# Two-column matmuls in place of small transposes, and another order of work around the adaLN modulation, in a one-core diffusion layer

## The chip, the cores and the metric

The kernel runs on one core of a Trainium2 chip. A core has TensorE (matmuls; in the profile PE, and PEld for its weight loads), VectorE (DVE), ScalarE (ACT), GpSimd (POOL) and SyncE (SP, which issues most transfers here). Each engine works through its own list of instructions in order, and the lists are tied together by semaphores. The metric is the device time of one execution in microseconds (us), as the median of several.

## The reference, cut to what matters

One layer of a diffusion backbone: an RMSNorm whose result is scaled and shifted by vectors computed from a conditioning vector (adaLN), one wide input projection, two attention branches, their merge and an output projection. There are 1024 latent tokens and 256 prompt tokens, 1024 features, all in f32. The change touches only the modulation at the start:

```python
def _modulation(cvec, w_ada, b_ada):
    m = jax.nn.silu(cvec) @ w_ada + b_ada
    return m[..., :D_MODEL], m[..., D_MODEL:2 * D_MODEL], m[..., 2 * D_MODEL:]   # shift, scale, gate

def _project(x, shift, scale, w_in):
    h = _rmsnorm(x) * (1.0 + scale) + shift
    p = h @ w_in
    ...
```

There are two conditioning vectors, one for the latent tokens and one for the prompt tokens, so every modulation value exists twice.

## The kernel before

Matrix products are done in split form. An f32 operand is written as a high part rounded to fp32r and a low part (the f32 value less the high part), and three fp32r matmuls (high by high, high by low, low by high) add up to the product (`split_mm`, L82 to L87, whose matmul is L86). ScalarE writes high parts, VectorE low parts.

The function `front` computes modulation, normalised activations, keys and values of branch B and the values of branch A. The order is written out by hand, one list for each engine:

- *Loads (SP).* A ring of eight 512 KB slots takes the adaLN weights (8 blocks of 128 rows for the shift half, 8 for the scale half), then the key weights, then six pieces of the value weights. Then come x tiles, tables and so on.
- *Modulation matmuls (TensorE, `modulation`).* With the SiLU of the two conditioning vectors as weights, blocks 0, 2, 4, 6 of each half go in split form (L313: four rows come out, namely the two products with the high parts of the vectors and the two with the low parts), and the others as ordinary f32 matmuls (L319: two rows). The results stand as 4 x 512 rows in two PSUM banks for each half: rows 0 and 1 the one sum, rows 2 and 3 the rest, for the two vectors.
- *Rows to columns (`columns`).* The modulation is needed with features along the partitions. ScalarE (L506, L514) and VectorE (L652) copy the rows to SBUF (`modrow`, shown in traces as h), TensorE transposes each 4 x 128 block to 128 x 4 (L334, into mod_ps), and VectorE adds the bias (L646, L655) and then columns 2 and 3 (L649, L659) into `modf`. columns(0) is the shift half, columns(1) the scale half.
- *Chunks.* For each of 8 feature blocks of a token group TensorE transposes the normalised x (`transposed`, L345, two banks in turn), ScalarE applies scale and shift (`modulate`, L453), VectorE writes high and low part (`parts`, L578 and L580), and TensorE runs the key matmuls of that block (`keys_chunk`, L353). ScalarE's chunk i waits for the low part of chunk i - 2, and x chunk i for ScalarE's chunk i - 2.
- *Value weights.* `values_high(m)` (ScalarE, L444) and `values_low(m)` (VectorE, L570) split the six pieces. The first value matmuls (`value_unit`, `split_mm`) need pieces 0 to 2 and all eight chunks.

The two semaphores that order this place are mod_row (rows copied to SBUF) and mod_col (a half transposed); mod_ready counts VectorE's adds into `modf`. After `front` come the attention pairs (`pairs`) and the merge (`finish`), which the change leaves alone.

Of the kernel before, what the change touches and what calls it, by code (L numbers as in the profile page):

```python
# [37 lines left out]
ALU = mybir.AluOpType  # L38
# [3 lines left out]
P = 128  # L42
D = 1024
KD = D // P
# [45 lines left out]
def front(nc, io, block, left, right, right_later, ident, scol, hm, wv, wkb, wt, wraw, craw, w_in, w_hi, w_lo):  # L90
# [12 lines left out]
    mod_ps, t_ps, k_ps, v_ps = (right_later[n] for n in ("mod_ps", "t_ps", "k_ps", "v_ps"))  # L103
    junk = left["junk"]
    scl = left["scl"]
    modrow = h32[0:4, :, :]
# [196 lines left out]
    @block.tensor  # L303
    def _(pe):
        def modulation(half, k):

            n = (SHIFT, SCALE)[half] + k
            if (half, k) in SPLIT:
                j = SPLIT.index((half, k))
                pe.wait_ge(mod_lo, j + 1)  # L310
                for c in range(2):
                    for part in range(2):
                        mm = pe.matmul(v_ps[0:4, 2 * half + c, :], scl[:, k, :], mod_part(j, part)[:, c * 512:(c + 1) * 512],  # L313
                                       start=(k == 0 and part == 0), stop=False, skip_group_check=True)
                mm.then_inc(ada_used, 1)
                return
            ring_wait(pe, n)
            for c in range(2):
                mm = pe.matmul(v_ps[0:2, 2 * half + c, :], scol[:, k, :], ring(n)[:, c * 512:(c + 1) * 512],  # L319
                               start=False, stop=(k == KD - 1), skip_group_check=True)  # L320
                if k == KD - 1:
                    mm.then_inc(mod_mm, 1)
            if k < KD - 1:
                mm.then_inc(ada_used, 1)

        def columns(half):

            if half == 1:
                pe.wait_ge(mod_ready, 2)
            for b in range(KD):  # L330
                if b % 4 == 0:
                    pe.wait_ge(mod_row, 2 * half + b // 4 + 1)
                blk = half * KD + b
                mm = pe.transpose(mod_ps[:, 4 * blk:4 * blk + 4], modrow[:, b // 4, (b % 4) * P:(b % 4 + 1) * P],  # L334
                                  ident[0:4, 0:4])
            mm.then_inc(mod_col, 1)

        def transposed(i):

            g, k = CHUNK[i]  # L340
            pe.wait_ge(xn_done, XG[g][0] + XG[g][1])
            if i >= 2:
                pe.wait_ge(h_done, i - 1)
            for t in range(XG[g][1]):
                mm = pe.transpose(t_ps[:, i % 2, t * P:(t + 1) * P], x(g)[:, t, k * P:(k + 1) * P], ident[:, :])  # L345
            mm.then_inc(xt_done, 1)

        def keys_chunk(g, k):

            t0, n = tokens(g)  # L350
            pe.wait_ge(lo_done, g * KD + k + 1)
            for i, (a, b) in enumerate(((0, 0), (0, 1), (1, 0))):
                mm = pe.matmul(k_ps[:, 0:n], wkb[:, a, k * P:(k + 1) * P], hm[:, b, k, t0:t0 + n],  # L353
                               start=(k == 0 and i == 0), stop=(k == KD - 1 and i == 2))
            if k == KD - 1:
                mm.then_inc(k_mm, 1)

        def value_unit(u):

            t, n = UNITS_V[u]  # L360
            if u == 0:
                pe.wait_ge(wv_lo, 3)
            if u == 4:
                pe.wait_ge(wv_lo, 6)
            pe.wait_ge(lo_done, KD * (1 if t < 4 else 2 if t < 8 else 3))
            if u >= 4:
                pe.wait_ge(v_lo, u - 3)
            split_mm(pe, v_ps[:, u % 4, 0:HW], lambda a, k: hm[:, a, k, t * P:(t + 1) * P],
                     lambda b, k: wv[:, b, k, n * HW:(n + 1) * HW], KD).then_inc(mm_done, 1)

        def gate_sum():

            pe.wait_ge(g_acc, 2 * KD)
            pe.wait_ge(const_set, 4)
            pe.wait_ge(h_done, len(CHUNK))
            for c in range(2):
                for s in range(2):
                    mm = pe.matmul(t_ps[0:2, c, :], pick[:, 2 * s:2 * s + 2], gacc[:, s, c * 512:(c + 1) * 512],
                                   start=(s == 0), stop=(s == 1))
            mm.then_inc(g_mm, 1)  # L380

        pe.wait_ge(scl_done, 2)
        for half, k in MODS:
            if (half, k) == (1, 6):
                pe.wait_ge(ident_in, 16)
                columns(0)
                transposed(0)
                transposed(1)
            modulation(half, k)
        columns(1)  # L390
        pe.wait_ge(wk_lo, 1)
        for k in range(KD):
            if k + 2 < KD:
                transposed(k + 2)
            keys_chunk(0, k)
        for u in range(3):
            value_unit(u)
        for j in range(4):
            transposed(KD + 2 * j)
            transposed(KD + 2 * j + 1)  # L400
            value_unit(3 + j)
        value_unit(7)
        pe.wait_ge(k_raw, 1)
        for k in range(KD):
            keys_chunk(1, k)
        for j in range(4):
            value_unit(8 + j)
            transposed(2 * KD + 2 * j)
            transposed(2 * KD + 2 * j + 1)
        for u in range(12, 16):  # L410
            value_unit(u)
        pe.wait_ge(k_raw, 2)
        for k in range(KD):
            keys_chunk(2, k)
        value_unit(16)
        value_unit(17)
        value_unit(18)
        gate_sum()
        value_unit(19)
        pe.wait_ge(k_raw, 3)  # L420
        pe.wait_ge(g_row, 2)

    @block.scalar
    def _(act):
# [16 lines left out]
        def values_high(m):  # L441

            ring_wait(act, VALUES + m)
            act.activation(values_split(m, 0), values_raw(m), ACT.Copy).then_inc(wv_hi, 1)  # L444

        def modulate(i):

            g, k = CHUNK[i]
            n, stream = XG[g][1] * P, int(g == 2)
            act.wait_ge(xt_done, i + 1)  # L450
            if i >= 2:
                act.wait_ge(lo_done, i - 1)
            act.activation(h32[:, i % 2, 0:n], t_ps[:, i % 2, 0:n], ACT.Identity,  # L453
                           bias=modf[:, k, stream:stream + 1], scale=modf[:, KD + k, stream:stream + 1]
                           ).then_inc(h_done, 1)
# [52 lines left out]
        ring_wait(act, KEYS)  # L508
        act.activation(wkb[:, 0, :], ring(KEYS), ACT.Copy).then_inc(wk_hi, 1)
        values_high(0)  # L510
        values_high(1)
        act.wait_ge(mod_mm, 3)
        act.wait_ge(mod_col, 1)
        act.activation(modrow[:, 0, :], v_ps[0:4, 2, :], ACT.Copy).then_inc(mod_row, 1)  # L514
        values_high(2)
        act.wait_ge(mod_ready, 4)
        for i in range(KD):
            modulate(i)
        for t in range(XG[1][1]):
            square(1, t)  # L520
        root(1)
# [25 lines left out]
    def _(dve):  # L547
# [19 lines left out]
        def values_low(m):  # L567

            dve.wait_ge(wv_hi, m + 1)
            dve.tensor_tensor(values_split(m, 1), values_raw(m), values_split(m, 0).bitcast(F32), ALU.subtract  # L570
                              ).then_inc(wv_lo, 1)
# [55 lines left out]
                    dve.scalar_tensor_tensor(out=gacc[:, s, :], in0=wgate(kg)[:, :], scalar=scol[:, kg, s:s + 1],  # L627
                                             in1=gacc[:, s, :], op0=ALU.mult, op1=ALU.add).then_inc(g_acc, 1)

        mods = mod_ps[:, 0:8 * KD].rearrange("p (b s) -> p b s", s=4)  # L630
        bias = bcol[:, :].rearrange("p (b o) -> p b o", o=1)
        dve.wait_ge(silu_done, 1)
        dve.tensor_copy(scl[:, :, 0:2], scol[:, :, :]).then_inc(scl_done, 1)
# [2 lines left out]
        for j in range(6):  # L636
# [2 lines left out]
        mod_low(7)  # L639
        dve.wait_ge(wk_hi, 1)  # L640
        dve.tensor_tensor(wkb[:, 1, :], ring(KEYS), wkb[:, 0, :].bitcast(F32), ALU.subtract).then_inc(wk_lo, 1)
        values_low(0)
        values_low(1)
        dve.wait_ge(small_in, 32)
        dve.wait_ge(mod_col, 1)
        dve.tensor_tensor(modf[:, 0:KD, :], mods[:, 0:KD, 0:2], bias[:, 0:KD, :].to_broadcast([P, KD, 2]), ALU.add  # L646
                          ).then_inc(mod_ready, 1)
        dve.wait_ge(mod_ready, 1)
        dve.tensor_tensor(modf[:, 0:KD, :], modf[:, 0:KD, :], mods[:, 0:KD, 2:4], ALU.add).then_inc(mod_ready, 1)  # L649
        dve.wait_ge(mod_mm, 4)  # L650
        dve.wait_ge(mod_row, 3)
        dve.tensor_copy(modrow[:, 1, :], v_ps[0:4, 3, :]).then_inc(mod_row, 1)  # L652
        values_low(2)
        dve.wait_ge(mod_col, 2)
        dve.scalar_tensor_tensor(out=modf[:, KD:, :], in0=mods[:, KD:, 0:2], scalar=1.0,  # L655
                                 in1=bias[:, KD:, :].to_broadcast([P, KD, 2]), op0=ALU.add, op1=ALU.add
                                 ).then_inc(mod_ready, 1)
        dve.wait_ge(mod_ready, 3)
        dve.tensor_tensor(modf[:, KD:, :], modf[:, KD:, :], mods[:, KD:, 2:4], ALU.add).then_inc(mod_ready, 1)  # L659
        for i in range(KD):  # L660
            parts(i)
        normalise(1)
        for m in range(3, 6):
            values_low(m)
# [1445 lines left out]
```

## Time and profile before

| | |
|---|---|
| median of 3 runs | 1246.5 us (1246.5 to 1248.01) |
| the profiled execution | 1246.5 us |
| its span, first to last instruction | 1244.7 us |
| mean granted TensorE clock | 0.995 |
| TensorE matmul busy | 1208.9 us (97%), 7488 instructions |
| TensorE weight loads | 1086.3 us (87%) |
| VectorE | 843.0 us (68%) |
| ScalarE | 613.5 us (49%) |
| GpSimd | 191.9 us (15%) |

Busy time is a share of the span. TensorE's weight loads overlap its matmuls. Matmuls are pipelined, so the duration of one is longer than the distance from its start to the next one's; where a price of one matmul is wanted, the distance between starts is the one to take. The chain of waits in the profile puts 75% of the span on TensorE and 13% on VectorE. In the profile's 40 slices TensorE is busy six tenths of the first (0 to 31 us), and nine tenths or more of all others but the last.

### The profile page before, as it was taken

The page shows a single profiled execution, that of the slowest core. Times are in us where ns is not written, and L with a number is a line of the kernel's source. Part 1 is how long each engine was busy: PE and PEld are TensorE (multiplying, and loading weights), DVE is VectorE, ACT ScalarE, POOL GpSimd, SP SyncE. Part 2 cuts the span into 40 slices and gives each one's busy share as a digit, 9 for nine tenths or more (in the row PEclk, how much of TensorE's full clock was granted, in tenths as well). Part 3 has the DMA queues.
Part 4 walks back from the last instruction along what each step waited for, and adds up shares of the span by engine and source line. Part 5 has one row for each costly group of instructions (what it writes and reads, how often), then busy time and mean ns, then how long its engine had stood idle before and what let it go on. Part 6 is the DMA issues. An engine that isn't in the chain of part 4 may idle for free.

```text
span 1244.7 us, 21419 instructions
## 1 busy us (share of the span) xinstructions
PE 1208.9 (97%) x7488; PEld 1086.3 (87%) x7488; DVE 843.0 (68%) x1654; ACT 613.5 (49%) x1217; POOL 191.9 (15%) x203
## 2 busy tenths in 40 slices
PE   6999999999999999999999999999999999999997
PEld 1699889988998998899889889989988888998996
DVE  3669458766766776687687687678768876454452
ACT  5532335534553555355466456555547574443341
POOL 0000214121302221141000000000000024533430
PEclk9999999999999999999999999999999999999999
DMA  9447523132214213222511111411013277543530
GB/s 365 146 185 219 202 88 102 58 133 83 93 62 136 87 63 121 84 93 76 168 62 39 54 56 39 126 43 62 18 51 111 72 238 250 174 151 115 200 138 34
DMA packets 81116, 143.03 MB, mean 115 GB/s; under 512 B 7047, under 2 KB 58119, under 8 KB 81037
## 3 DMA queue, kind: packets, MB, share of 16 engines
q1 hardware_dynamic: 66636, 119.92, 28.9%
q10 hardware_dynamic: 14400, 22.15, 4.9%
q8 instruction: 38, 0.62, 0.2%
q14 instruction: 42, 0.34, 0.1%
HBM read 106.65 MB, written 35.40 MB: 114 GB/s over the span
## 4 chain that ended last, share of the span: by engine, by line
PE 75%; DVE 13%; issue 5%; ACT 4%; DMA 2%; ACTq 0%; SPq 0%; DVEq 0%; POOL 0%
PE d_ps_pairs L86 20%; PE y_ps L1836 9%; PE b_ps L86 9%; PE s_ps_pairs L86 8%; PE o_ps_pairs L1069 7%; PE t_ps_pairs L1038 6%; PE v_ps L86 6%; PE s_ps_pairs L997 3%; PE s_ps_pairs L996 3%; DVE pt L1388 2%; DVE mn L1398 1%; DVE s_ps_pairs L1405 1%; PE k_ps L353 1%; ACT pr L1194 1%; DVE pr L1454 1%
## 5 line engine op out<-in xcount | busy, mean ns | idle before, releaser
L86 PE MATMUL d_ps_pairs<-h,wt 128*128 128x384 f32 (+2 forms) x1920 | 352.3, 338 | 0.5 <-ACT craw L1212 0.5
L86 PEld LDWEIGHTS d_ps_pairs<-h,wt 128*128 128x128 f32 x1920 | 316.7, 188 | 15.6 <-ACT craw L1212 1.0
L1388 DVE TENSOR_TENSOR pt<-t_ps_pairs,pt 128x512 fp32r<-128x512 f32 (+1 forms) x272 | 157.6, 621 | 38.7 <-ACT pt L1170 37.4
L86 PE MATMUL s_ps_pairs<-h,wt 128*128 128x512 f32 (+1 forms) x864 | 169.3, 355 | 0.5 <-DVE q L1345 0.5
L1194 ACT ACTIVATE pr<-s_ps_pairs,mx 128x896 f32<-128x896 f32 x128 | 128.3, 1005 | 70.3 <-DVE mx L1414 40.8
L86 PEld LDWEIGHTS s_ps_pairs<-h,wt 128*128 128x128 f32 x864 | 141.7, 189 | 23.0 <-DVE q L1345 1.1
L1170 ACT ACTIVATE pt<-t_ps_pairs 128x512 fp32r<-128x512 f32 (+1 forms) x272 | 134.1, 548 | 14.7 <-PE t_ps_pairs L1038 9.9
L1038 PE MATMUL t_ps_pairs<-ident_sb,pr 128*128 128x128 f32 x960 | 131.7, 275 | 4.0 <-DVE pt L1388 2.8
L1038 PEld LDWEIGHTS t_ps_pairs<-ident_sb,pr 128*128 128x128 f32 x960 | 107.7, 140 | 15.7 <-DVE pt L1388 11.4
L1836 PE MATMUL y_ps<-wo,mg 128*128 128x512 f32 x480 | 113.2, 396 | 0.0
L1790 POOL TENSOR_TENSOR tp<-tp 128x256 f32<-128x256 f32 x40 | 32.3, 808 | 497.7 <-DVE tp L1888 497.1
L1836 PEld LDWEIGHTS y_ps<-wo,mg 128*128 128x128 f32 x480 | 90.0, 188 | 21.6
L1398 DVE TENSOR_REDUCE mn<-s_ps_pairs 128x2 f32<-128x1024 f32 x64 | 78.1, 1220 | 36.3 <-PE s_ps_pairs L997 35.0
L947 POOL TENSOR_TENSOR comb_a<-rowm_a,comb_a 128x384 f32<-128x384 f32 x48 | 45.4, 945 | 318.1 <-DMA comb_a<-in_bias 318.1
L86 PE MATMUL b_ps<-og,wb 128*128 128x256 f32 x720 | 87.7, 282 | 1.6 <-DVE tp L1888 1.6
L86 PEld LDWEIGHTS b_ps<-og,wb 128*128 128x128 f32 x720 | 86.8, 188 | 1.9 <-DVE wb L1565 1.0
L1454 DVE TENSOR_SCALAR pr<-pr,rden 128x896 f32<-128x896 f32 x128 | 87.0, 722 | 2.2
L1243 ACT ACTIVATE otmp<-o_ps_pairs 64x256 f32<-64x256 f32 (+1 forms) x72 | 29.2, 405 | 117.0 <-PE o_ps_pairs L1069 116.5
L1212 ACT ACTIVATE craw<-d_ps_pairs 128x384 f32<-128x384 f32 (+2 forms) x80 | 39.0, 488 | 74.5 <-PE d_ps_pairs L86 74.4
L86 PE MATMUL v_ps<-wv,h 128*128 128x320 f32 x480 | 73.1, 310 | 0.0
L86 PEld LDWEIGHTS v_ps<-wv,h 128*128 128x128 f32 x480 | 70.7, 188 | 1.0 <-issue 0.9
L1888 DVE TENSOR_TENSOR tp<-b_ps,gt 128x256 f32<-128x256 f32 x80 | 31.9, 420 | 46.0 <-PE b_ps L86 33.2
(184 smaller groups left out, 1722.3 us busy)
## 6 DMA issues: line engine op xcount, KB each, us to landing
wraw<-in_w_gate SPq DMA_DIRECT2D x24, 512.0 KB, 3.4
gt<-gates_d SPq DMA_DIRECT2D x40, 256.0 KB, 4.5
comb_a<-in_bias SPq DMA_DIRECT2D x24, 384.0 KB, 3.6
gates_d<-craw ACTq DMA_DIRECT2D x48, 192.0 KB, 1.9
vw_a<-v_d SPq DMA_DIRECT2D x64, 128.0 KB
v_d<-vst SPq DMA_DIRECT2D x20, 320.0 KB, 4.5
wada<-in_w_ada SPq DMA_DIRECT2D x12, 512.0 KB, 8.8
oz<-gates_d SPq DMA_DIRECT2D x20, 256.0 KB, 4.7
```

Source lines behind the costliest of these rows:

```text
L86: mm = eng.matmul(out, lhs(a, k), rhs(b, k), start=(k == 0 and i == 0), stop=(k == n_k - 1 and i == 2))
L947: pool.tensor_tensor(c, rm, c, ALU.subtract).then_inc(comb_t, 1)
L996: pe.matmul(out, cols(q1[:, h, :]), rhs(h, slice(0, P)), start=True, stop=False)
L1038: mm = pe.transpose(t_ps[:, n % 2, b * P:(b + 1) * P], probs_block(s, t, kb), ident[:, :])
L1069: mm = pe.matmul(o_ps[:, c0 * P:(c0 + nb) * P], v, pt[:, part, b0 * P:(b0 + nb) * P], start=(half == 0 and part == 0 and (n == 0 or (s == ...
L1170: act.activation(pt[:, 0, c * 512:c * 512 + cols], t_ps[:, n % 2, 0:cols], ACT.Copy).then_inc(hi_done, 1)
L1194: act.activation(probs_run(s, t), scores_run(s, t), ACT.Exp, bias=mx[:, t:t + 1], scale=-1.0, accum_out=den[:, t:t + 1]).then_inc(exp_done, 1)
L1212: act.activation(gst[:, u % 2, 0:n], d_ps[:, 0:n], ACT.Copy).then_inc(g_done, 1)
L1388: dve.tensor_tensor(pt[:, 1, c * 512:c * 512 + cols], t_ps[:, n % 2, 0:cols], pt[:, 0, c * 512:c * 512 + cols].bitcast(F32), ALU.subtract) ...
L1398: dve.tensor_reduce(mn[:, 0:2], s_ps[:, :, :].rearrange("p (t b) c -> p t b c", b=2)[:, :, s % 2, :], AX.X, ALU.min).then_inc(m1_done, 1)
L1454: dve.tensor_scalar(probs_run(s, t), probs_run(s, t), rden[:, t:t + 1], None, ALU.mult).then_inc(p_done, 1)
L1836: mm = pe.matmul(y_ps[:, e, n * 512:(n + 1) * 512], mg[:, a, k, e * P:(e + 1) * P], wo[k][:, b, n * 512:(n + 1) * 512], start=(k == 0 and ...
```

## The change

In `columns`, each 4 x 128 block is no longer transposed by the transpose operation with the 4 x 4 identity. Two matmuls with two columns of the identity each write the same two columns of mod_ps, the second adding to the first; so rows 0 and 2, and 1 and 3, are summed in PSUM. VectorE's two adds L649 and L659 go, with the waits around them. The order around it changes in all three lists.

```diff
             if half == 1:
-                pe.wait_ge(mod_ready, 2)
+                pe.wait_ge(mod_ready, 1)
...
-                mm = pe.transpose(mod_ps[:, 4 * blk:4 * blk + 4], modrow[:, b // 4, (b % 4) * P:(b % 4 + 1) * P],
-                                  ident[0:4, 0:4])
+                for part in range(2):
+                    mm = pe.matmul(mod_ps[:, 2 * blk:2 * blk + 2], modrow[:, b // 4, (b % 4) * P:(b % 4 + 1) * P],
+                                   ident[0:4, 2 * part:2 * part + 2], start=(part == 0), stop=(part == 1))
...
                 columns(0)
-                transposed(0)
-                transposed(1)
             modulation(half, k)
+        transposed(0)
         columns(1)
+        transposed(1)
...
         values_high(0)
-        values_high(1)
         act.wait_ge(mod_mm, 3)
         act.wait_ge(mod_col, 1)
         act.activation(modrow[:, 0, :], v_ps[0:4, 2, :], ACT.Copy).then_inc(mod_row, 1)
-        values_high(2)
-        act.wait_ge(mod_ready, 4)
+        values_high(1)
+        act.wait_ge(mod_ready, 2)
         for i in range(KD):
             modulate(i)
+            if i == 1:
+                values_high(2)
...
-        values_low(0)
-        values_low(1)
         dve.wait_ge(small_in, 32)
         dve.wait_ge(mod_col, 1)
-        dve.tensor_tensor(modf[:, 0:KD, :], mods[:, 0:KD, 0:2], bias[:, 0:KD, :].to_broadcast([P, KD, 2]), ALU.add
+        dve.tensor_tensor(modf[:, 0:KD, :], mods[:, 0:KD, :], bias[:, 0:KD, :].to_broadcast([P, KD, 2]), ALU.add
                           ).then_inc(mod_ready, 1)
-        dve.wait_ge(mod_ready, 1)
-        dve.tensor_tensor(modf[:, 0:KD, :], modf[:, 0:KD, :], mods[:, 0:KD, 2:4], ALU.add).then_inc(mod_ready, 1)
         dve.wait_ge(mod_mm, 4)
         dve.wait_ge(mod_row, 3)
         dve.tensor_copy(modrow[:, 1, :], v_ps[0:4, 3, :]).then_inc(mod_row, 1)
-        values_low(2)
         dve.wait_ge(mod_col, 2)
-        dve.scalar_tensor_tensor(out=modf[:, KD:, :], in0=mods[:, KD:, 0:2], scalar=1.0,
+        dve.scalar_tensor_tensor(out=modf[:, KD:, :], in0=mods[:, KD:, :], scalar=1.0,
                                  in1=bias[:, KD:, :].to_broadcast([P, KD, 2]), op0=ALU.add, op1=ALU.add
                                  ).then_inc(mod_ready, 1)
-        dve.wait_ge(mod_ready, 3)
-        dve.tensor_tensor(modf[:, KD:, :], modf[:, KD:, :], mods[:, KD:, 2:4], ALU.add).then_inc(mod_ready, 1)
+        values_low(0)
+        values_low(1)
         for i in range(KD):
             parts(i)
+        values_low(2)
```

TensorE's list, from the last but one split modulation block of the scale half to the first key matmuls, before (v_ps holds modulation rows, mod_ps the modulation in columns, t_ps the transposed x, k_ps the keys):

```order
L313 MATMUL v_ps<-h,scl 4x512 x4
L334 MATMUL mod_ps<-ident_sb,h 128x4 x8
L345 MATMUL t_ps<-ident_sb,x 128x128 x8
L313 MATMUL v_ps<-h,scl 4x512 x4
L319 MATMUL v_ps<-x,scol 2x512 x2
L334 MATMUL mod_ps<-ident_sb,h 128x4 x8
L345 MATMUL t_ps<-ident_sb,x 128x128 x4
L353 MATMUL k_ps<-h,wkb 128x512 x3
```

and the same place now:

```order
L313 MATMUL v_ps<-h,scl 4x512 x4
L335 MATMUL mod_ps<-ident_sb,h 128x2 x16
L313 MATMUL v_ps<-h,scl 4x512 x4
L319 MATMUL v_ps<-x,scol 2x512 x2
L346 MATMUL t_ps<-ident_sb,x 128x128 x4
L335 MATMUL mod_ps<-ident_sb,h 128x2 x16
L346 MATMUL t_ps<-ident_sb,x 128x128 x8
L354 MATMUL k_ps<-h,wkb 128x512 x3
```

Each set of 8 has become 16 instructions, and the first two x chunks have moved from ahead of the last two modulation blocks to either side of the second set.

VectorE's list from the key weights' low part to the first chunk, before (wkb key weights, wv value weights, modf the modulation, h as output of L652 the copied rows and of L578 and L580 the parts of the chunk):

```order
L641 TENSOR_TENSOR wkb<-wada,wkb 128x1024
L570 TENSOR_TENSOR wv<-wada,wv 128x3x320 x2
L646 TENSOR_TENSOR modf<-mod_ps,bcol 128x16
L649 TENSOR_TENSOR modf<-modf,mod_ps 128x16
L652 COPY h<-v_ps 4x512
L570 TENSOR_TENSOR wv<-wada,wv 128x2x320
L655 SCALAR_TENSOR_TENSOR modf<-mod_ps,bcol 128x16
L659 TENSOR_TENSOR modf<-modf,mod_ps 128x16
L578 CAST h<-h 128x512
```

and now:

```order
L643 TENSOR_TENSOR wkb<-wada,wkb 128x1024
L646 TENSOR_TENSOR modf<-mod_ps,bcol 128x16
L650 COPY h<-v_ps 4x512
L652 SCALAR_TENSOR_TENSOR modf<-mod_ps,bcol 128x16
L572 TENSOR_TENSOR wv<-wada,wv 128x3x320 x2
L580 CAST h<-h 128x512
L582 TENSOR_TENSOR h<-h 128x512
```

The first two value weight pieces moved from ahead of L646 to between the last add and the first chunk; the third now stands behind the last of the eight chunks.

## Rows read from the trace of the kernel before

**Rows 1.** Chain of waits: start us, us, what.

```profile
33.88 0.58 PE mod_ps L334 x8
...
38.94 0.73 DVE wv L570
...
52.55 10.57 PE v_ps L86 x72
```

**Rows 2.** Timeline, TensorE: start us, us, instruction, [idle before it <- released by].

```profile
33.81 0.65 PE L334 MATMUL mod_ps<-ident_sb,h 4*128 4x4 f32 x8
34.39 1.09 PE L345 MATMUL t_ps<-ident_sb,x 128*128 128x128 f32 x8
35.24 1.17 PE L313 MATMUL v_ps<-h,scl 128*4 128x512 f32 x4
...
38.15 0.40 PE L334 MATMUL mod_ps<-ident_sb,h 4*128 4x4 f32 x4
...
42.01 1.65 PE L353 MATMUL k_ps<-h,wkb 128*128 128x512 f32 x3 [0.47 <-DVE h L580]
...
45.47 0.60 PE L345 MATMUL t_ps<-ident_sb,x 128*128 128x128 f32 x4
45.83 0.94 PE L353 MATMUL k_ps<-h,wkb 128*128 128x512 f32 x3
...
46.96 0.95 PE L353 MATMUL k_ps<-h,wkb 128*128 128x512 f32 x3
47.75 0.60 PE L345 MATMUL t_ps<-ident_sb,x 128*128 128x128 f32 x4
...
52.39 10.73 PE L86 MATMUL v_ps<-wv,h 128*128 128x320 f32 x72
```

**Rows 3.** The same timeline, VectorE.

```profile
33.78 1.16 DVE L570 TENSOR_TENSOR wv<-wada,wv 128x960 fp32r<-128x960 f32 x1
...
38.26 0.68 DVE L652 COPY h<-v_ps 4x512 f32<-4x512 f32 x1 [1.68 <-PE v_ps L319]
...
39.60 0.15 DVE L655 SCALAR_TENSOR_TENSOR modf<-mod_ps,bcol 128x16 f32<-128x16 f32 x1
39.79 0.17 DVE L659 TENSOR_TENSOR modf<-modf,mod_ps 128x16 f32<-128x16 f32 x1
40.80 0.43 DVE L578 CAST h<-h 128x512 fp32r<-128x512 f32 x1 [0.85 <-ACT h L453]
...
50.84 0.69 DVE L580 TENSOR_TENSOR h<-h 128x512 fp32r<-128x512 f32 x1
55.30 0.18 DVE L552 RECIPROCAL rstd<-rms 128x4 f32<-128x4 f32 x1 [3.76 <-ACT rms L438]
...
58.17 2.22 DVE L570 TENSOR_TENSOR wv<-wada,wv 128x960 fp32r<-128x960 f32 x2
60.31 0.82 DVE L570 TENSOR_TENSOR wv<-x,wv 128x640 fp32r<-128x640 f32 x1
```

**Rows 4.** The same timeline, ScalarE.

```profile
37.40 0.59 ACT L514 ACTIVATE h<-v_ps 4x512 f32<-4x512 f32 x1 [2.30 <-PE v_ps L319]
37.89 0.72 ACT L444 ACTIVATE wv<-wada 128x640 fp32r<-128x640 f32 x1
39.99 1.45 ACT L453 ACTIVATE h<-t_ps,modf 128x512 f32<-128x512 f32 x2 [1.38 <-DVE modf L659]
```

**Rows 5.** Busy time by stretch, behind the first value matmul: stretch, length, engines, clock, DMA.

```profile
52.40:130.00 77.60, 77.60 (x533) 76.47 (x532) 57.60 (x95) 28.53 (x55) 0.00 (x0) 1.00 0.50 163
```

**Rows 6.** Line L319, its matmul records: duration ns min/median/max, first and last start, forms.

```profile
L319 PE MATMUL v_ps<-wada,scol x24: 591/592/1015, 9.7 to 32.3; 128*2 128x512 f32 x24
...
L319 PE MATMUL v_ps<-x,scol x8: 591/592/592, 23.6 to 37.6; 128*2 128x512 f32 x8
```

**Rows 7.** Busy time by stretch, around the first key matmul.

```profile
38.55:42.00 3.45, 1.03 (x9) 0.74 (x8) 2.54 (x7) 1.51 (x3) 0.00 (x0) 0.99 1.02 408
42.00:45.40 3.40, 3.39 (x10) 2.78 (x11) 2.06 (x5) 1.55 (x2) 0.00 (x0) 0.51 0.23 89
```

More of the change, by code:

```diff
@@ L628, in gate_product @@
                                              in1=gacc[:, s, :], op0=ALU.mult, op1=ALU.add).then_inc(g_acc, 1)
-        mods = mod_ps[:, 0:8 * KD].rearrange("p (b s) -> p b s", s=4)
+        mods = mod_ps[:, 0:4 * KD].rearrange("p (b s) -> p b s", s=2)
         bias = bcol[:, :].rearrange("p (b o) -> p b o", o=1)
```

## The prediction

> **What bounds the kernel now.** I read the chain of waits first. It runs through the whole span, and up to the first key projection its links are one serial line: the load of the adaLN weights, TensorE's modulation matmuls, then in turn ScalarE, VectorE and TensorE with little on any of them. The part that the change touches lies in it piece by piece (some of them in [rows 1]): the eight small transposes of L334, the eight x transposes of L345, the last modulation matmuls (L319), VectorE's row copy (L652), a weight split (L570, 0.73 us) that only stands in front of L655 in VectorE's queue, then L655, L659, ScalarE's first modulated chunk (L453), VectorE's two parts of it (L578, L580) and the first key matmuls at 42.01. Second I read the timelines of TensorE, VectorE and ScalarE over 33 to 53 us [rows 2 to 4], for who is late where. Third I looked at what follows: from 52.4 to 130 us TensorE is busy the whole time [rows 5], and everything else waits for it or has room. So whatever the front loses or wins ahead of the first value matmul (52.39) moves the rest as a block, and reaches the end: after that point nothing in the order changes. The profiled execution took 1246.5 us, which is the median of the three; its span is 1244.7, so 1.8 us lie outside.
>
> **What the edits are, priced one at a time.** I name moments by the trace before and carry a shift d.
>
> 1. *First set of small products, columns(0).* Before: 8 transposes, from 33.81 to the next start at 34.39: 0.58 us, 0.0725 each with their 4x128 weight load [rows 2]. Now each block is two ordinary f32 matmuls of two columns, which add the high and low rows in PSUM: 16 matmuls. The trace shows what an ordinary f32 matmul costs in records: L319 issues two per k over 8 such k, which is 16, and the two rows of L319 count 24 + 8 = 32 [rows 6]. So 16 matmuls are 32 weight loads and 32 array passes, where a transpose was one record. No row shows such a record at 128x2. Bounds: from above the 128x128 transpose of L345, 0.85 us for 8 or 0.106 each, which loads 128 weight columns and streams 128; farther above, L86 at 10.57/72 = 0.147 [rows 1]; from below, the pair of records at the price of one L334, 0.036 each. L334 itself has the same weights (4 rows, 128 columns) and nearly no moving columns, so I take 0.0725: 32 x 0.0725 = 2.32 us, +1.74. It is on the path, because TensorE runs without an idle time from 33.81 to 38.15.
>
> 2. *x transposes moved behind the modulation matmuls.* The 8 of L345 at 34.39 took 0.85 us ahead of the last two modulation steps [rows 2]: -0.85. The last modulation result, which VectorE waited for at 38.26, now comes at 38.26 + 1.74 - 0.85 = 39.15; TensorE's stream behind it goes on at 39.04 (38.15 before).
>
> 3. *Second set, columns(1).* transposed(0) now stands ahead of it: 4 of those transposes, 0.43 us, to 39.47. The first half needs ScalarE's row copy (L514, 0.59 us [rows 4]), which shifts by 0.89 to end at 38.88; the second needs VectorE's (L652, 0.68), 39.15 to 39.83; TensorE comes to it at 39.47 + 1.16 = 40.63. Neither waits. 32 x 0.0725 = 2.32 ends at 41.79; with 0.07 for the last pass to finish and 0.04 to hand over, L655 starts at 41.90. Before it started at 39.60 and was followed by L659; L659 goes (-0.19 from start to start), and so does the split of 0.73 us in front of L655. The modulation is ready at 42.05 against 39.96, and ScalarE's first chunk starts at 42.08 against 39.99: d = +2.09. The three savings (0.85, 0.73, 0.19) are real but come to 1.77 us against 3.9 us more of matmul records.
>
> 4. *Two weight splits moved behind L655.* values_low(0) and (1) ran at 33.78 and 35.13, while VectorE had nothing to do: it sat idle 1.68 us before L652 [rows 3]. Now they stand between L655 and the parts of the first chunk. Two such splits take 2.14 us from the start of one pair to what follows it (58.17 to 60.31 [rows 3]). From 42.03 they end at 44.17; the first chunk is ready from ScalarE at 42.08 + 0.81 = 42.89 (39.99 to 40.80 before) and waits 1.3 us. The cast L578 starts at 44.17 against 40.80: d = +3.4. Queued behind it are the keys' first matmuls, which need L580, and ScalarE's third chunk, which needs the same. The first key matmul moves from 42.01 to 45.4.
>
> 5. *The rest costs nothing.* ScalarE's values_high(1) (half as wide again as values_high(2), which took 0.72 [rows 4], so about 1.1 us) goes into its wait between L514 and the modulation (38.9 to 42.1); uncovered it would cost 1.1. values_high(2) goes behind chunk 1, where ScalarE waits for L580 of chunk 0 anyway: chunk 1 ends near 43.6, that L580 near 45.4. VectorE's values_low(2) (0.80) now follows the last parts, which ended at 50.84 + 0.69 = 51.53, ready by 52.33; the first value matmul, which needs it, started at 52.39 after the last key chunk. That is a tie, at most +0.1. VectorE then waited 3.76 us for ScalarE's L438 [rows 3], so normalise(1) isn't late. L646 drops its follower L649 (0.20), off the path. The loads keep their order, and none of their releases depends on a moved instruction.
>
> Key chunks 0 to 7 took 42.01 to 52.39. Their pace is set by TensorE, ScalarE and VectorE in turn and nothing in their order changes, so d = +3.4 passes through: 1246.5 + 3.4 = **1249.9 us**, +0.27%.
>
> The row of L334 speaks against a rule of the skill: eight weight loads of 128 columns and eight passes went by in 0.58 us [rows 2]. The Trainium skill (TensorE: Matmul & The Clock Gate, "LDWEIGHTS (loading the stationary operand)") puts a weight load at the number of columns over 1.2, whatever the rows, which would be 107 ns here and more than the measured 72.5 ns for load and pass together. By that rule the sum would be about 1252, an estimate, as in the dear case below; by the row it is 1249.9.
>
> **Rivals.**
>
> *The clock holds through the key chunks.* Granted clock was 0.51 from 42.0 to 45.4, after 3.45 us in which TensorE was busy 1.03 [rows 7]; so the first two key chunks and the transposes between them ran at the 1.2 GHz level: 42.01 to 45.47 is 3.46 us, where the same three pieces one lap later (key chunk 46.96 to 47.75, transposes 45.47 to 45.83) are 0.79 + 0.36 + 0.79 = 1.94 [rows 2]. Now TensorE works from 39.04 to about 42.8 and then idles some 2 us before the first key matmul. For: TensorE idles less than in the 3.45 us that went before the fall here. Against: there is still a gap, and the passes are tiny. If it holds, 1.5 us come back: d = +1.9, 1248.4, which is no change. This is the case on the other side: its place is the stretch of 42 to 48 us, its price 1.5, and it decides as soon as it gives back over 0.9 us. With cheap records (next but one) on top d would be -0.45, 1246.0.
>
> *The small matmuls are dear.* At L345's 0.106 each set costs 1.07 more, both lie on the path: d = +3.4 + 2.1 = +5.5, 1252.0; at L86's 0.147, +8.2, 1254.7. For: two passes accumulate into the same two columns right behind each other, which the trace nowhere shows, and the clock may be at 1.2 GHz in part of them. Against: L334.
>
> *The small matmuls are cheap* (a pair for the price of one transpose, so the edit costs no TensorE time): each set 1.16 us less. The modulation would then be ready at 39.7, 0.2 before its old time, but the two splits still stand in the way: d = +3.4 - 2.3 = +1.1, 1247.6, no change.
>
> **Chances.** Forecast (d from 2.6 to 4.6) 0.52; clock holds 0.17; dear 0.16; cheap 0.08; cheap with the clock held, or something as good, 0.04; elsewhere 0.03. About 0.2% of the time, 2.5 us, is what a measurement can tell from no change. Slower: 0.52 + 0.16 + 0.03 = 0.71. The same: 0.17 + 0.08, less 0.01 for a part of them that goes lower still: 0.24. Faster: that 0.01 and the 0.04, 0.05 in all, since only these come near it. The range is 1247.5 (cheap) to 1252.8 (past L345's price): it leaves out the far end of the dear case and what lies under the cheap one. The forecast's own range is 1249.1 to 1251.1.
>
> **What the profile of the changed kernel would show.** Step 1: 32 records in the first set, about 2.3 us from its first start to the next matmul; 1.2 says cheap, 3.4 says dear. Step 2: VectorE's row copy near 39.2. Step 3: second set ends near 41.8, the one remaining add of the scale half starts near 41.9 and ScalarE's first chunk near 42.1. Step 4: two splits of 1.16 us between that add and the first cast, the cast near 44.2, while ScalarE's chunk 0 had ended 1.3 us earlier. Step 5: first key matmul near 45.4, first value matmul near 55.8, with no wait there for the split of VectorE; clock near 0.5 for some 3 us from the first key matmul on. I am wrong if the first value matmul comes within 2 us of 52.4, or if it comes at 55.8 and the end does not move with it, which would mean room later that I took for none.

## The result, and the profile after

The changed kernel took 1255.57 us (median, 1253.78 to 1256.91) against 1246.5 before: 1.0070 of the time, 95% interval 1.0052 to 1.0088, about 9 us slower. The forecast was slower too, but by 3.4 us, with a range that ended at 1252.8. The direction was right and the size wrong. The profiled execution took 1256.8 us (before: 1246.5), its span is 1254.9 us (1244.7).

TensorE's timeline after, at the place of [rows 2] (start us, us, instruction, records, idle before it):

```profile
33.20 1.09 PE L313 MATMUL v_ps<-h,scl 128*4 128x512 f32 x4
34.21 4.51 PE L335 MATMUL mod_ps<-ident_sb,h 4*128 4x2 f32 x32
38.65 1.87 PE L313 MATMUL v_ps<-h,scl 128*4 128x512 f32 x4
40.45 3.52 PE L319 MATMUL v_ps<-x,scol 128*2 128x512 f32 x4
43.90 0.66 PE L346 MATMUL t_ps<-ident_sb,x 128*128 128x128 f32 x4
44.49 4.54 PE L335 MATMUL mod_ps<-ident_sb,h 4*128 4x2 f32 x32
48.96 2.33 PE L346 MATMUL t_ps<-ident_sb,x 128*128 128x128 f32 x8
52.49 1.65 PE L354 MATMUL k_ps<-h,wkb 128*128 128x512 f32 x3 [1.21 <-DVE h L582]
...
63.61 2.69 PE L86 MATMUL v_ps<-wv,h 128*128 128x320 f32 x17
```

Each set has the 32 records that were foretold, but takes 4.44 and 4.47 us from start to start, not 2.32. And the modulation matmuls between the sets, which the change doesn't touch, take 5.25 us (38.65 to 43.90) where they took 2.91 (35.24 to 38.15 in [rows 2]). The granted clock tells why (busy time by stretch; the number after the five engines is the clock):

```profile
34.20:36.70 2.50, 2.50 (x24) 2.49 (x23) 0.00 (x0) 0.00 (x0) 0.00 (x0) 1.00 1.04 341
37.20:38.60 1.40, 1.40 (x8) 1.40 (x7) 0.00 (x0) 0.00 (x0) 0.00 (x0) 0.50 1.08 392
38.65:43.90 5.25, 5.25 (x9) 0.68 (x9) 0.17 (x1) 1.48 (x2) 0.00 (x0) 0.51 0.86 348
44.50:46.90 2.40, 2.40 (x23) 2.40 (x22) 0.19 (x1) 0.00 (x0) 0.00 (x0) 1.00 0.00 0
47.20:48.90 1.70, 1.70 (x10) 1.70 (x9) 0.00 (x0) 0.00 (x0) 0.00 (x0) 0.50 0.00 0
```

Inside each set the clock falls to its 1.2 GHz level, although TensorE is busy all the time (2.50 of 2.50 us before the fall, 1.40 of 1.40 behind it). After the first set the long modulation matmuls pay for it. VectorE, the place of [rows 3]:

```profile
38.83 0.17 DVE L646 TENSOR_TENSOR modf<-mod_ps,bcol 128x16 f32<-128x16 f32 x1 [4.99 <-PE mod_ps L335]
44.01 0.68 DVE L650 COPY h<-v_ps 4x512 f32<-4x512 f32 x1 [5.00 <-PE v_ps L319]
49.06 0.17 DVE L652 SCALAR_TENSOR_TENSOR modf<-mod_ps,bcol 128x16 f32<-128x16 f32 x1 [4.38 <-PE mod_ps L335]
49.15 2.22 DVE L572 TENSOR_TENSOR wv<-wada,wv 128x960 fp32r<-128x960 f32 x2
51.29 0.42 DVE L580 CAST h<-h 128x512 fp32r<-128x512 f32 x1
```

and ScalarE, of [rows 4]:

```profile
42.35 0.59 ACT L514 ACTIVATE h<-v_ps 4x512 f32<-4x512 f32 x1 [8.49 <-PE v_ps L319]
42.84 0.99 ACT L445 ACTIVATE wv<-wada 128x960 fp32r<-128x960 f32 x1
49.27 1.62 ACT L454 ACTIVATE h<-t_ps,modf 128x512 f32<-128x512 f32 x2 [5.44 <-DVE modf L652]
50.79 0.73 ACT L445 ACTIVATE wv<-wada 128x640 fp32r<-128x640 f32 x1
```

At each turn VectorE waits 4.4 to 5.0 us, and ScalarE 8.5 and 5.4 us: for TensorE's small matmuls, for what stands behind them, or for the add that waited for them. The two splits (L572) lie between the last add and the first cast as foretold.

### The profile page after: what moved, and what is told of

Its sections match the earlier page's. It is cut to its first block, busy times and chain, and to the rows that moved or that the text cites. A ratio compares the mean times of both kernels' runs of the same rounds, so it can differ in the third digit from the quotient of the medians.

```text
span 1254.9 us, 21513 instructions
## 1 busy us (share of the span) xinstructions
PE 1221.5 (97%) x7536; PEld 1095.1 (87%) x7536; DVE 843.2 (67%) x1652; ACT 613.6 (49%) x1217; POOL 192.1 (15%) x203
## 4 chain that ended last, share of the span: by engine, by line
PE 78%; DVE 12%; issue 4%; ACT 4%; DMA 1%; ACTq 0%; SPq 0%; DVEq 0%; POOL 0%
PE d_ps_pairs L86 19%; PE s_ps_pairs L86 11%; PE y_ps L1834 9%; PE b_ps L86 9%; PE o_ps_pairs L1067 7%; PE t_ps_pairs L1036 6%; PE v_ps L86 6%; PE s_ps_pairs L995 3%; PE s_ps_pairs L994 3%; DVE pt L1386 2%; DVE mn L1396 1%; DVE s_ps_pairs L1403 1%; ACT pr L1192 1%; PE v_ps L319 1%; PE k_ps L354 1%
```

## The experiments

Medians are compared with before's on the same chip (1246.24, 1246.13 and 1246.05 us in the three groups of runs). Single executions of before lie between 1243.1 and 1248.4, so a single execution tells a clock or the distance between two records, not a microsecond of total time. A good part of that spread arises before the change's place: in the thirteen profiles the first set of small products starts between 32.40 and 35.42 us, and what differs is the clock from 18 to 24 us. Where it stayed at 1.00 the set starts at 32.40 to 32.60 (four profiles); in the kernel before, with 0.50 and 0.64 over 18 to 22 us, at 33.81. Two profiles of one and the same kernel start it at 34.07 and 35.42. So the place is best compared from the start of its first set: up to the first value matmul it takes 18.58 us before (33.81 to 52.39) and 29.40 us after (34.21 to 63.61).

**The two halves of the change.** Matmuls alone: the edit of `columns` with VectorE's two adds gone, all orders as before.

> The order of before, with only the arithmetic of the change: two accumulating two-column f32 matmuls a block in place of one transpose, without VectorE's two adds. Theory A (the matmul records are the whole of it: 0.107 us each at the full clock and 0.21 at half, against 0.0725 for a transpose, and the modulation matmuls behind the first set then run at half clock too): the first set takes 3.4 to 4.5 us, the two modulation steps behind it about 5.3 instead of 2.9, the second set 3.4 or more; 7 to 10 us over before, about 1255, nearly all of the 9 us of the full change. Theory B (the new order costs the most, the split weights in front of the first chunk and x transposes in the wrong place): under 4 us over before, below 1250.5.

Order alone: the reverse.

```diff
-                for part in range(2):
-                    mm = pe.matmul(mod_ps[:, 2 * blk:2 * blk + 2], ...
+                mm = pe.transpose(mod_ps[:, 4 * blk:4 * blk + 4], ...
```

> The order of the change in all three lists, with the transposes and VectorE's four adds of before. Theory A: the modulation is ready about 1.1 us earlier, the two splits give back 1.3, so within 0.5 us of before, about 1246.8. Theory B (order): 4 us or more over before.

Measured: matmuls alone 1255.76 (1.0069, interval 1.0046 to 1.0091), order alone 1246.62 (1.0007, 0.9997 to 1.0016). The matmuls are the whole loss within what can be measured, and the order as a whole is free, because two of its parts cancel. In its profile ScalarE's first chunk starts 5.11 us after the first set (33.99 to 39.10) where it took 6.18 before (33.81 to 39.99), 1.07 less; then the two splits hold up the first cast, which comes 7.13 us after the set's start (41.12) against 6.99.

The single executions of the matmuls alone reach from 1248.86 us, at a mean granted clock of 0.997, to 1258.17 us, at 0.991. That is a spread of 9.3 us against 3.8 of before on the same chip: how much clock is lost differs from run to run. In its profile the sets take 4.34 and some 4.7 us.

**The place of the splits.** The full change with

```diff
         values_high(0)
+        values_high(1)
...
+        values_low(0)
+        values_low(1)
         dve.wait_ge(small_in, 32)
...
-        values_low(0)
-        values_low(1)
         for i in range(KD):
```

> The full change, but with the two value weight splits back ahead of the adds on VectorE, and the ScalarE half of the second ahead of the row copy. Step 4 of the prediction put 1.3 us on their place, and the trace after shows the first cast 1.2 us after its chunk is ready: 1.2 us faster than the changed kernel, about 1254.3. Rival: the key chunks run at half clock and TensorE is late anyway, so nothing comes back, 1255.6.

Measured 1254.17, but its ratio is 1.0076 (1.0059 to 1.0093) where the full change has 1.0070: inconclusive as a time. The trace is plain: the first cast comes 1.02 us after the last add instead of 2.23 (49.06 to 51.29). It reaches the first key matmul, which starts 2.33 us behind the second set (45.78 to 48.11) instead of 3.53 (48.96 to 52.49), which speaks against the rival.

```profile
45.88 0.18 DVE L654 SCALAR_TENSOR_TENSOR modf<-mod_ps,bcol 128x16 f32<-128x16 f32 x1 [4.35 <-PE mod_ps L335]
46.90 0.43 DVE L580 CAST h<-h 128x512 fp32r<-128x512 f32 x1 [0.84 <-ACT h L454]
```

This run also has a first set with the clock full to its end: 32.58 to 36.24, 3.66 us or 0.114 a record. The fall comes behind it, in L319:

```profile
32.58 3.73 PE L335 MATMUL mod_ps<-ident_sb,h 4*128 4x2 f32 x32
36.24 1.09 PE L313 MATMUL v_ps<-h,scl 128*4 128x512 f32 x4
37.26 3.56 PE L319 MATMUL v_ps<-x,scol 128*2 128x512 f32 x4
```

**What a record costs, and why.** Half as many of them, without accumulation, in the kernel before:

```diff
-                mm = pe.transpose(mod_ps[:, 4 * blk:4 * blk + 4], ..., ident[0:4, 0:4])
+                mm = pe.matmul(mod_ps[:, 4 * blk:4 * blk + 4], ..., ident[0:4, 0:4], start=True, stop=True)
```

> Order and adds of before, with one ordinary f32 matmul of four columns a block in place of the transpose (8 a set, so 16 records). Theory A1 (each record is bound by its weight load, 0.107 us at full clock): a set takes 1.7 us, 1.1 more than before, 2 to 4 us over before in all, about 1249. Theory A2 (the second matmul's accumulation into the same two columns is what is slow, the rest costs like a transpose): 16 records at 0.0725, 0.6 more a set, about 1247.5.

Measured 1248.32. One of the ten executions took 2060 us, at a mean granted clock of 0.592 against 0.994 to 0.996 in the others; what held its clock down is open. Without it the median is 1248.02, and the ratio 1.0014 (1.0000 to 1.0027). A set of 16 records took 1.88 us (34.75 to 36.63), 0.1175 each, with a full clock behind the first set, through the modulation matmuls:

```profile
34.75 1.94 PE L334 MATMUL mod_ps<-ident_sb,h 4*128 4x4 f32 x16
36.63 1.09 PE L345 MATMUL t_ps<-ident_sb,x 128*128 128x128 f32 x8
```

So accumulation isn't what is dear. Two matmuls a block without it confirm that:

```diff
-                mm = pe.transpose(mod_ps[:, 4 * blk:4 * blk + 4], ...
+                for part in range(2):
+                    mm = pe.matmul(mod_ps[:, 4 * blk + 2 * part:4 * blk + 2 * part + 2], ..., start=True, stop=True)
```

> Order and VectorE's adds of before; two ordinary f32 matmuls of two columns a block as in the change, but into separate columns, none adding to the other (32 records a set, nothing accumulated). Theory A1 (the weight load is the price of a record): 0.107 us a record at full clock as with accumulation, the clock falls as there, about 1255.8 as with the accumulating matmuls. Theory A2 (accumulating into the same columns is dear): records near 0.0725, about 1250.

Measured 1254.67 (1.0078, 1.0052 to 1.0104), as with accumulation, and 3.66 us for the first set (33.91 to 37.57), again 0.114 a record. Next, as many records of the cheap kind, each block transposed four times:

```diff
-                mm = pe.transpose(mod_ps[:, 4 * blk:4 * blk + 4], ...
+                for rep in range(4):
+                    mm = pe.transpose(mod_ps[:, 4 * blk:4 * blk + 4], ...
```

> Order and adds of before, each block transposed four times over into the same place, so 32 transpose records a set. It tells the number of records from their kind. Theory A1 (an ordinary f32 matmul's weight load is dearer than a transpose's): 0.0725 us each, 2.3 us a set. If short records by themselves make the clock fall, both sets and the modulation matmuls between show the half clock: 6 us or more over before, 1252.5. If the kind of record does, the clock is full there: about 3.5 us over before, 1249.8.

Measured 1249.1 (1.0027, 1.0017 to 1.0037). A set of 32 took 2.06 us, 0.064 each, all of it at full clock; but the clock fell right behind it, into the x transposes and the modulation step:

```profile
32.60:34.60 2.00, 2.00 (x33) 2.00 (x32) 1.88 (x2) 1.34 (x3) 0.00 (x0) 1.00 1.08 363
34.60:37.50 2.90, 2.90 (x14) 2.02 (x13) 1.92 (x4) 0.68 (x1) 0.00 (x0) 0.53 1.10 369
```

So a series of short records, transposes too, can be followed by the half clock; neither of my two readings in the expectation (clock full, or half in everything between) fits. Last, ordinary matmuls that are not f32: the rows rounded to fp32r as they are copied, into a free part of hm.

```diff
+    modr = lambda c: hm[0:4, 1, 2 * c:2 * c + 2, LAT:TOK]
...
+                    mm = pe.matmul(mod_ps[:, 2 * blk:2 * blk + 2], hm[0:4, 1, b // 2, ...], identr[:, 2 * part:2 * part + 2], ...
```

> Order of before with the accumulating two-column matmuls, but on fp32r operands: the copied rows are rounded to fp32r as they are written (so the modulation loses low bits, which is the part of the computation that changes), and the identity's four columns are copied once. 16 fp32r matmuls a set, one record each. Theory A1 (an ordinary f32 matmul is two records with a slow weight load each, the kind is what costs): 16 records at 0.07 us or a little more, 1.2 us a set, clock full, 0.5 to 1.5 us over before, about 1247. Rival (any matmul that isn't a transpose loads at 0.11 here): as the 16 records of the single f32 matmul, 1.9 us a set, 1248.3.

Measured 1248.91 (1.0027, 1.0015 to 1.0038), and 16 records in 1.87 us (32.40 to 34.27), 0.117 each:

```profile
32.40 1.94 PE L337 MATMUL mod_ps<-h 4*128 4x2 f32 x16
34.27 1.09 PE L348 MATMUL t_ps<-ident_sb,x 128*128 128x128 f32 x8
```

Here my theory fell and its rival held. It isn't f32 that makes a record slow: the small ordinary matmuls tried (128 weight columns, few streamed columns) took 0.114 to 0.118 us a record, a transpose of the same 4 x 128 block 0.064 to 0.073. That it is f32 only doubles the number of records.

**Does streaming more columns hold the clock?** 126 columns of the identity instead of 2 in the full change.

```diff
-    mod_ps[:, 2 * blk:2 * blk + 2], ..., ident[0:4, 2 * part:2 * part + 2]
+    mod_ps[:, 2 * blk:2 * blk + 126], ..., ident[0:4, 2 * part:2 * part + 126]
```

> The full change, but each of its small matmuls streams 126 columns of the identity in place of 2 (the further columns hold nothing that is used and are overwritten by the next block). Theory A1 (weight load and streaming overlap, and the load, 128 columns at 0.107 us, is the price): the record costs the same 0.107 at full clock. If the clock stays full with the array streaming, the 3.5 us that the half clock cost come back, about 1252; if it falls as before, 1255.6. Rival (the record's price is load plus stream): 0.21 a record, 6.8 us a set, 1259 or more.

Its profile showed the clock at 1.00 through both sets and all between (34.07 to 45.00), and a set at 3.76 us, 0.1175 a record: 63 times as many columns cost next to nothing, so the price isn't the streaming. What is left is the weight load or another cost of each record. The weight loads' own records differ as the prices do, a median of 187 ns for the ordinary matmul here and of 137 for the transpose of the same block four times over, and in both the loads follow each other without a gap (busy 3.64 of 3.66 us in the third experiment's first set, 2.00 of 2.00 in the transposes'):

```profile
L335 PEld LDWEIGHTS mod_ps<-ident_sb,h x64: 181/187/188, 34.1 to 44.7; 4*128 4x128 f32 x64
...
L335 PEld LDWEIGHTS mod_ps<-ident_sb,h x64: 133/137/140, 32.6 to 41.9; 4*128 4x128 f32 x64
```

(records of duration ns min/median/max, first and last start; the first line is of the wide columns, the second of the transposes four times over). That points to the weight load, but no run changed the number of weight columns, so it isn't shown.

The median was 1255.91 (1.0085, 1.0069 to 1.0101), no better than the change. Each of the two kernels was profiled once more:

> The full change with 126 streamed columns once more, for its clock alone. If streaming keeps the clock up, both sets and the modulation matmuls between them show 1.0 again, a set takes 3.8 us and the L313 step behind it 1.0; if the first profile was luck, the half clock shows in a set or right behind it.

> The changed kernel once more, for its clock alone. If the two-column records bring the clock down, the last part of a set and the modulation matmuls behind the first show 0.5 again, wherever the start falls; if its first profile was bad luck, they show 1.0 and the time is near 1252.

The wide one took 1260.29 us, with the clock at half in the very place; its first profile was luck:

```profile
34.41 1.09 PE L313 MATMUL v_ps<-h,scl 128*4 128x512 f32 x4
35.42 4.59 PE L335 MATMUL mod_ps<-ident_sb,h 4*128 4x126 f32 x32
39.94 1.87 PE L313 MATMUL v_ps<-h,scl 128*4 128x512 f32 x4
41.74 3.55 PE L319 MATMUL v_ps<-x,scol 128*2 128x512 f32 x4
```

The change once more took 1257.56 us, with sets of 4.85 and 4.87 us and again 1.87 for the L313 step behind the first. What the narrow matmuls lose in clock repeats in the second profile, its size varies, and wide columns don't cure it.

The lucky profile is worth more than it seems, since it shows the new matmuls with a full clock through both sets and all between. From the start of the first set to the first value matmul it takes 25.41 us (34.07 to 59.48). The same kernel with the clock fallen takes 29.62 (35.42 to 65.04), and the change 29.40 and 29.43: the clock costs 4.0 to 4.2 us there. The order alone, with transposes, takes 18.78 (33.99 to 52.77), so the records at full clock cost 6.6. These are single executions.

**A version that beats both.** The order-alone kernel with the two splits put back ahead; against the kernel before:

```diff
                 columns(0)
-                transposed(0)
-                transposed(1)
             modulation(half, k)
+        transposed(0)
         columns(1)
+        transposed(1)
...
-        values_high(2)
         act.wait_ge(mod_ready, 4)
         for i in range(KD):
             modulate(i)
+            if i == 1:
+                values_high(2)
...
-        values_low(2)
         dve.wait_ge(mod_col, 2)
...
             parts(i)
+        values_low(2)
```

> The version that the runs so far point to: transposes and VectorE's four adds of before, value weight splits 0 and 1 where they were, but the x transposes behind the last modulation matmuls, and the third split behind the last chunk. The first cast comes 1.05 us earlier than before (transposes 0.85 off the path, the split of 0.73 out of the way, less a wait for TensorE): 1245.2 by the trace. Rival: the idle stretch ahead of the key chunks stays and the half clock moves with it, so nothing shows at the end, 1246.3.

Measured 1243.86 us (0.9981, 0.9971 to 0.9990): faster than before by 1.2 to 3.6 us. In its profile the way from the first set to the first cast is 6.47 us (32.57 to 39.04) against 6.99 (33.81 to 40.80), only 0.5 shorter, because the second split holds up the row copy:

```profile
35.28 1.16 DVE L571 TENSOR_TENSOR wv<-wada,wv 128x960 fp32r<-128x960 f32 x1 [0.19 <-ACT wv L444]
36.36 0.17 DVE L647 TENSOR_TENSOR modf<-mod_ps,bcol 128x16 f32<-128x16 f32 x1
36.56 0.17 DVE L650 TENSOR_TENSOR modf<-modf,mod_ps 128x16 f32<-128x16 f32 x1
36.65 0.67 DVE L653 COPY h<-v_ps 4x512 f32<-4x512 f32 x1
39.04 0.43 DVE L579 CAST h<-h 128x512 fp32r<-128x512 f32 x1 [0.84 <-ACT h L453]
```

From the first set to the first value matmul it takes 18.13 us (32.57 to 50.70) against 18.58, again 0.45 less. Its first set starts 1.24 us earlier than before's, ahead of all that was changed, where the clock was 1.00 from 18 to 24 us. The mean granted clock of its eleven executions is 0.997 in the median, against 0.996 in before's twenty. That the median gains 2.3 us where the place explains 0.5 stays open. Against the third experiment, which differs from it only in `columns` and the adds, the matmuls cost 1254.17 - 1243.86 = 10.3 us (the two ran in different groups; before's medians there differ by 0.1).

## Why the prediction was wrong in size

*Step 1, the price of a small record, is the step that failed*, and with it a term that the sum put at nothing, the half clock in and behind the sets. The profiled execution lost 10.3 us and not 3.4. Of the 6.9 between them the price of a record is 2 x (3.66 - 2.32) = 2.7, and the clock 4.0 (29.40 less the 25.41 of the profile with a full clock there).

*The price.* I took 0.0725 us, from L334, because it has the same weights. Measured: 0.114 to 0.118 at full clock. The count of 32 was right. At full clock the first set costs 3.66 us, +3.1 and not +1.74. The nearest row was not the one with the same shape of weights but the one bound above, L345's 0.106, and even that was a little low. The Trainium skill's rule on weight loads (TensorE: Matmul & The Clock Gate, "LDWEIGHTS (loading the stationary operand)"), the number of columns over 1.2 whatever the rows, so an estimate of 107 ns for 128 columns, comes within about 10% of the ordinary matmuls here (114 to 118 ns), and not of the transposes (64 to 73 ns); I had tested it on a transpose and set it aside.

*The clock.* The rival with the clock only asked whether the old half-clock stretch would go. The reverse took place: the fall came earlier, in the middle of the set. In the profile after, the first set's 4.44 us hold 4.44 - 3.66 = 0.78 of it, and the untouched modulation matmuls behind it 5.25 - 2.91 = 2.34. I had named half clock inside the small matmuls as a reason for the dear case, and put no price on what stands behind them.

*Step 2* was right: the L313 step follows the set directly, -0.85. TensorE's stream behind the modulation came at 43.90 against 38.15, +5.75; that is +0.40 at the start of the first set, +3.86 in it, -0.85, +2.34. The 0.40 arose ahead of the change's place, where the half clock came and went later in this execution (0.67 over 22 to 24 us, against 1.00 before).

*Step 3*: neither row copy was waited for, as foretold; the second set cost 4.47 instead of 2.32 and transposed(0) 0.59 instead of 0.43. ScalarE's first chunk started at 49.27 against 39.99, +9.28, where I had +2.09.

*Step 4* was right: the first cast moved by 10.49, 1.21 more than the chunk, against the 1.3 forecast. *Step 5*: both ScalarE splits and values_low(2) cost nothing visible, and the order alone measures 1.0007. But the key chunks took 11.12 us (52.49 to 63.61) against 10.38, since the half clock, 3.4 us of it before [rows 7], lasted longer here, 4.8 us from the first key matmul (0.50 from 52.49 to 57.30).

The first value matmul came 11.22 us late and the profiled execution was 10.3 late. The last of that is not the block shift I expected: the loads of the cached keys, one for each pair of heads, come 11.54, 10.94 and 10.36 us later than before in branch A and 10.31 at the first pair of branch B, near which the distance stays to the end (10.2 of span). The loop of branch A gave back 1.2 us; which of its waits did so I didn't test. From the first value matmul to the end of the execution, where no list differs, the thirteen profiled executions take 1192 to 1196 us (1194.1 before, 1193.2 after), so a difference of a microsecond there needs no cause in the change.

```profile
254.65 0.34 SPq L868 DMA_DIRECT2D craw<-in_cka  x1
...
601.08 0.33 SPq L868 DMA_DIRECT2D craw<-in_ckb  x1
```

is before (SP's timeline), and after:

```profile
266.19 0.34 SPq L866 DMA_DIRECT2D craw<-in_cka  x1
...
611.39 0.33 SPq L866 DMA_DIRECT2D craw<-in_ckb  x1
```

In sum, of the 10.3 us between the third experiment and the best version, 2 x (3.66 - 0.58) = 6.2 are records at full clock, and the remaining 4 I put down to the clock. Of the medians that split is worked out, not shown, for no run had the matmuls and a clock that reliably stays up. The one profile that had both, with wide columns, gives much the same, 6.6 and 4.2. Why the clock falls in or behind such a set stays open: the runs show when it does, and that neither wide columns nor transposes prevent it.

## What to carry to other kernels

Price a new instruction by a row of the same kind (ordinary matmul or transpose), not only of the same shape, and where none exists let the higher bound weigh more. Saving two 0.17 us adds on VectorE is not worth 48 more records on TensorE where TensorE is on the path. A series of short matmuls can cost as much behind itself as in itself (32 transposes in place of 8: 1.5 us in the set, 1.6 behind it): look at the granted clock of what follows.

## What the runs showed of the hardware

- A 4 x 128 block as weights of an ordinary matmul: 0.114 to 0.118 us from record to record at full clock, the same for f32 and fp32r, for 2, 4 or 126 streamed columns, with and without accumulation. At half clock it is about 0.21, an estimate: in the profile after, the clock fell near 37.0, 2.8 us into the set, which is 24 records at 0.114, and the other 8 took 1.7 us. The same block in a transpose, at full clock: 0.064 (32 in a row) to 0.073 (8). That the ordinary one is dearer by its weight load is likely, not shown. An ordinary f32 matmul is two such records, an fp32r one is one.
- TensorE's clock fell from its 2.4 GHz to its 1.2 GHz level while the engine was busy without a gap, in the first set of 32 short records or within 1.1 us behind it, in seven of the eight profiles of kernels with such sets. It did so neither in nor behind the first set of 16 records (two profiles) or of 8 transposes (three profiles), up to the last modulation matmul.
- The same kernel differs between executions in whether and where this happens: with wide columns once not at all (clock 1.00 from 34.07 to 45.00) and once in the first set; for matmuls alone the mean granted clock goes from 0.997 to 0.991 and the time from 1248.86 to 1258.17 us.
